# Retention's sums of squares as two float32r products of a high and a low part with ones

## The reference

```python
def head_layernorm(y):
    mu = jnp.mean(yf, axis=-1, keepdims=True)
    var = jnp.mean((yf - mu) ** 2, axis=-1, keepdims=True)
    return (yf - mu) * lax.rsqrt(var + EPS)
...
q = rope(q.reshape(B, S, H, d), cos, sin)
k = rope(k.reshape(B, S, H, d), cos, sin) * (d ** -0.5)
y_ret = head_layernorm(retention_chunkwise(q, k, v, log_gamma)).reshape(B, S, RET_WIDTH)
y_a = (jax.nn.silu(g_ret) * y_ret) @ ret_w_out[l]
```

## Time and profile before

| | us |
|---|---|
| median of 3 runs | 2533.19 (2532.08 to 2534.12) |
| the profiled execution | 2532.75 |
| its span, first to last instruction | 2531.0 |
| retention stage, first head's first score to the last head's root | about 1605 to 1821 |

### The profile page before, as it was taken

One profiled execution on the slowest core, in us unless ns is written; L12 is line 12 of the kernel. 1 busy time (PEld: TensorE's weight loads), 2 busy tenths in 40 slices (PEclk: granted clock), 3 DMA queues, 4 the chain that ended last, 5 costly groups with the idle time before them and its releaser, 6 DMA issues.

```text
span 2531.0 us, 35040 instructions
## 1 busy us (share of the span) xinstructions
PE 2474.6 (98%) x13577; PEld 2236.6 (88%) x13593; DVE 1825.4 (72%) x3334; ACT 1064.8 (42%) x1585; POOL 483.3 (19%) x344
## 2 busy tenths in 40 slices
PE   8999899999999999999999999999999999999998
PEld 6788888899999998999999999787788888888887
DVE  7876577999999989688888887787786335533323
ACT  6555366345555555333333335444422223422222
POOL 3222165033322353233333310000000000000000
PEclk9999999999999999999999999999999999999999
DMA  4211344588988899999999983222275333233231
GB/s 167 68 60 43 117 142 160 182 305 329 331 302 301 309 398 365 362 377 365 367 368 364 363 315 128 75 84 96 93 265 188 100 100 108 75 100 98 89 105 42
DMA packets 191236, 519.12 MB, mean 205 GB/s; under 512 B 15896, under 2 KB 67096, under 8 KB 187872
## 3 DMA queue, kind: packets, MB, share of 16 engines
q1 hardware_dynamic: 154208, 382.66, 43.2%
q0 software_dynamic: 36864, 134.23, 14.6%
HBM read 464.34 MB, written 52.49 MB: 204 GB/s over the span
## 4 chain that ended last, share of the span: by engine, by line
PE 81%; DVE 11%; DMA 4%; ACT 3%; issue 2%; SPq 0%; DVEq 0%; ACTq 0%
PE P L1240 25%; PE P L1242 25%; PE P L1241 24%; DMA GB<-un,SI 3%; DVE wl L1696 2%; PE P L1584 1%; PE P L1247 1%; DVE GB L2000 1%; ACT wh L2326 1%; DVE T L1696 1%; DVE D L1696 1%; DVE RQ L2211 0%; DVE RW L1696 0%; DVE RU L1696 0%; DVE OE L1696 0%
## 5 line engine op out<-in xcount | busy, mean ns | idle before, releaser
L1240 PE MATMUL P<-XH,wh 128*128 128x512 f32 (+2 forms) x2272 | 851.1, 375 | 9.4 <-DVE wl L1696 6.7
L1242 PE MATMUL P<-XH,wl 128*128 128x512 f32 (+2 forms) x2272 | 824.8, 363 | 0.0
L1241 PE MATMUL P<-XL,wh 128*128 128x512 f32 (+2 forms) x2272 | 824.2, 363 | 0.0
L1696 DVE TENSOR_TENSOR wl<-raw,wh 128x1024 fp32r<-128x1024 f32 x418 | 506.4, 1219 | 39.5 <-ACT wh L2326 39.5
L2326 ACT ACTIVATE wh<-raw 128x1024 fp32r<-128x1024 f32 x458 | 480.7, 1052 | 127.2 <-PE P L1242 125.7
L1240 PEld LDWEIGHTS P<-XH,wh 128*128 128x128 f32 x2272 | 429.3, 189 | 56.4 <-DVE wl L1696 10.3
L1242 PEld LDWEIGHTS P<-XH,wl 128*128 128x128 f32 x2272 | 428.2, 188 | 48.0
L1241 PEld LDWEIGHTS P<-XL,wh 128*128 128x128 f32 x2272 | 429.2, 189 | 42.5 <-issue 1.9
L1240 PE MATMUL P<-AH,wh 128*128 128x384 f32 x1024 | 343.7, 336 | 2.2 <-DVE wl L1696 1.7
L1242 PE MATMUL P<-AH,wl 128*128 128x384 f32 x1024 | 342.2, 334 | 0.0
L1241 PE MATMUL P<-AL,wh 128*128 128x384 f32 x1024 | 342.2, 334 | 0.0
(11 more groups left out here) (326 smaller groups left out, 3211.1 us busy)
## 6 DMA issues: line engine op xcount, KB each, us to landing
raw<-wts SPq DMA_DIRECT2D x211, 512.0 KB, 3.6
raw<-ut SPq DMA_DIRECT2D x128, 512.0 KB, 6.6
raw<-vt SPq DMA_DIRECT2D x128, 512.0 KB, 9.7
hdram<-HID SPq DMA_DIRECT2D x64, 384.0 KB, 4.7
gdram<-GS SPq DMA_DIRECT2D x24, 1024.0 KB, 6.3
GI<-gdram SPq DMA_DIRECT2D x16, 1536.0 KB, 13.1
HI<-hdram SPq DMA_DIRECT2D x32, 768.0 KB, 11.8
AWC<-adat SPq DMA_DIRECT2D x64, 256.0 KB, 5.4
```

Of the source, the lines that this page charges most:

```text
L1240: e.matmul(bank, wh[:, w], H, start=start, stop=False)
L1241: e.matmul(bank, wh[:, w], L, start=False, stop=False)
L1242: return e.matmul(bank, wl[:, w], H, start=False, stop=stop)
L1696: return e.tensor_tensor(dst, a, b, op)
```

## The change

`r_root`'s product with ones is no longer one float32 matmul but two in float32r that add up in the same bank: ones x high part and ones x low part of the squares. So:

- ScalarE, in `r_values`, after the square: it waits for its own square and copies `RSQ` to `RSQH` (float32r).
- VectorE, in a new piece `r_square`: it waits for that copy and subtracts, `RSQL` = `RSQ` - `RSQH`, in place of `RSQ`. In head 0 it also copies `ones` to `onesr` (128x128) once.
- TensorE, in `r_root`: it waits for `RSQL` instead of `RSQ`, then two matmuls.
- `retain` hands out `r_root` 6.4 tiles behind `r_values` instead of 5.2; the way from `r_values` to the end of the head stays 11.0 tiles.
- `RSQH` takes the place of `SRL`'s first part in memory, so VectorE's first `SRL` of a head also waits for the head before's sums.

```diff
--- before.py
+++ after.py
@@ -643,9 +643,11 @@
             yield ("r_low", h, 3)
             yield 6.0
             yield ("r_values", h)
-            yield 5.2
+            yield 3.0
+            yield ("r_square", h)
+            yield 3.4
             yield ("r_root", h)
-            yield 4.4
+            yield 3.2
             yield ("r_factor", h, 0)
             yield ("r_factor", h, 1)
             yield 1.4
@@ -885,6 +887,9 @@
         SRL = at("SRL", F + 85, [128, 1280], F32R)
         DM = [at(f"DM{i}", F + 94 + 2 * i, [128, T], F32) for i in range(2)]
         RSQ = at("RSQ", F + 98, [128, T], F32)
+        RSQL = at("RSQL", F + 98, [128, T], F32R)
+        RSQH = at("RSQH", F + 85, [128, T], F32R)
+        onesr = at("onesr", F + 100, [128, 128], F32R)
         R1 = TB[4]
 
 
@@ -969,7 +974,7 @@
         s_rope, s_qrh, s_qrl, s_rcopy = sem("s_rope"), sem("s_qrh"), sem("s_qrl"), sem("s_rcopy")
         s_rt, s_rcen, s_vrh, s_vrl, s_silu = sem("s_rt"), sem("s_rcen"), sem("s_vrh"), sem("s_vrl"), sem("s_silu")
         s_rsc, s_rdm, s_srh, s_srl = sem("s_rsc"), sem("s_rdm"), sem("s_srh"), sem("s_srl")
-        s_rval, s_rsq, s_rg, s_rones = sem("s_rval"), sem("s_rsq"), sem("s_rg"), sem("s_rones")
+        s_rval, s_rsq, s_rg, s_rsql, s_rones = sem("s_rval"), sem("s_rsq"), sem("s_rg"), sem("s_rsql"), sem("s_rones")
         s_rroot, s_rq = sem("s_rroot"), sem("s_rq")
         s_ry, s_rh, s_rl = sem("s_ry"), sem("s_rh"), sem("s_rl")
 
@@ -1648,8 +1653,9 @@
                     p.wait_ge(s_rroot, h)
                 else:
                     p.wait_ge(s_silu, 1)
-                p.wait_ge(s_rsq, h + 1)
-                e.matmul(P[5][:, :], ones[:, :], RSQ[:, :], start=True, stop=True).then_inc(s_rones, 1)
+                p.wait_ge(s_rsql, h + 1)
+                e.matmul(P[5][:, :], onesr[:, :], RSQH[:, :], start=True, stop=False)
+                e.matmul(P[5][:, :], onesr[:, :], RSQL[:, :], start=False, stop=True).then_inc(s_rones, 1)
 
             def down(m, k, u, c, half):
                 if c == 0:
@@ -2192,6 +2198,8 @@
                 w = T - 128 * kb
                 q = slice(offs[kb], offs[kb + 1])
                 v.wait_ge(s_srh, n + 1)
+                if h and kb == 0:
+                    v.wait_ge(s_rones, h)
                 tt(SRL[:, q], TB[5 + n % 2][:, 0:w], SRH[:, q].bitcast(F32), ALU.subtract).then_inc(s_srl, 1)
 
             def r_first(k):
@@ -2202,8 +2210,14 @@
             def r_values(h):
                 sg = TB[2 + h % 2]
                 v.wait_ge(s_silu, h + 1)
-                v.wait_ge(s_rsq, h + 1)
+                v.wait_ge(s_rsq, 2 * h + 1)
                 tt(sg[:, :], P[4][:, :], sg[:, :], ALU.mult).then_inc(s_rg, 1)
+
+            def r_square(h):
+                if h == 0:
+                    e.tensor_copy(onesr[:, :], ones[:, :])
+                v.wait_ge(s_rsq, 2 * h + 2)
+                tt(RSQL[:, :], RSQ[:, :], RSQH[:, :].bitcast(F32), ALU.subtract).then_inc(s_rsql, 1)
 
             def r_factor(h, half):
                 w = cols(half)
@@ -2310,7 +2324,7 @@
                 constants, slopes, gained, low, root, norm, norm_low, masks, forget, scaled, qk_split, v_copy, v_turn, soft, normal, turn_low,
                 values, mixed, subkeys, query, top, places, candidates, pair, gate, chosen, index, gate_turn, iotas, hot, weigh, angle,
                 rotation, rotation_end, mod_part, mod_end, rows, sparse_index, dot, dots_end, axpy, second, sum2, first_norm, rope, r_turn,
-                r_decay, r_low, r_first, r_values, r_factor, r_end, conv_begin, conv, merge_a, merge_b, merged, remixed,
+                r_decay, r_low, r_first, r_values, r_square, r_factor, r_end, conv_begin, conv, merge_a, merge_b, merged, remixed,
                 ffn_up, added, stored)}
             work |= {"sum": sum_, "activate": activate_}
             for name, *a in timeline():
@@ -2614,6 +2628,8 @@
                 if h:
                     c.wait_ge(s_rones, h)
                 e.activation(RSQ[:, :], P[4][:, :], ACT.Square).then_inc(s_rsq, 1)
+                c.wait_ge(s_rsq, 2 * h + 1)
+                copy(RSQH[:, :], RSQ[:, :]).then_inc(s_rsq, 1)
 
             def r_root(h):
                 c.wait_ge(s_rones, h + 1)
```

## The result

| | before | after |
|---|---|---|
| median of 20 runs each, us | 2533.31 | 2537.73 |
| the profiled execution, us | 2532.75 | 2535.82 |
| its span, us | 2531.0 | 2534.0 |
| from head 0's square to the end of the span, us | 905.55 | 909.25 |

The changed kernel takes 1.0021 of the time (95% interval 1.0015 to 1.0027). It is slower: the interval leaves out no change. The forecast was 2536.7, with the remark that such a loss would most likely be too small to be told from none; twenty runs of each kernel can just tell it.

The account below looks back on a forecast made before the run. ScalarE and VectorE, handing work round at 27.62 us per head, bound the retention, not TensorE. 3.45 + 1.58 - 0.68 - 0.41 = 3.9, less 0.2 in head 7, gives +3.7: 2536.7 us, 8-in-10 range 2533.5 to 2539.5.

Parts of the forecast that it names:

- The ring of ScalarE and VectorE: Retention heads: the two engines hand work to each other in a closed loop that sets the pace, 27.62 us per head.
- Rival 1: Retention: TensorE is the bound after all and keeps 3.3 us, time 2529.9, or 2528.4 without its waits; chance 0.10.
- VectorE's part: The added subtraction, pushing a weight unit by 0.60 us, falls into VectorE's 1.30 us wait for the root and costs nothing.
- The ring's growth: ScalarE's added copy lengthens each period from heads 1 to 5 by 0.69 us (bounds 0.54 and 0.88), 3.45 in all.
- Behind head 6: TensorE's work after head 6's sums: start 1.58 us later, less 0.68 for the moved tile and 0.41 for shorter products.
- The products: TensorE's sums in each head: two float32r products take 0.46 us instead of 0.87, a gain of 0.41.
- rival 3: Products with the float32r ones go at float32 pace, 1.28 us more per head than forecast, time 2539.3; chance 0.02.
- Head 0: ScalarE's copy of v there waits 1.46 us for TensorE, which covers the new copy, so no growth behind it.
- Head 7: Not paced by the other two engines: TensorE waits 0.2 us, saves 0.41, so 0.2 us gained.
- TensorE's waits: In front of the sums in each head, TensorE's wait becomes about 1.5 us, now for VectorE's `RSQL`.
- rival 2: The new waits let TensorE's clock fall, up to 7.9 us slower, 2539 to 2541; chance 0.10 that it decides.
- TensorE's own work: TensorE's work per head without waits: 27.24 us before, falling to 26.83, not what sets the pace.

Follow-up runs that it names:

- The copy alone: Kernel before plus only ScalarE's copy of the squares to float32r, unused, the sums still one float32 product; 2537.17 us (1.0010).
- one product: Changed kernel with squares written rounded to float32r, low part left out, one float32r product at its old place; 2532.28 us (0.9997).
- the move alone: Kernel before with only the sums product one tile later in TensorE's order; 2535.22 us (1.0004).
- the move undone: Changed kernel with the sums product back at its old place in TensorE's order; 2536.34 us (1.0007).
- the swap in before: Kernel before with each head's first-unit weight copy (ScalarE) and subtraction (VectorE) one tile later, behind the first masked scores; 2530.49 us (0.9986).
- the rounding on VectorE: Changed kernel with the high part of the squares copied by VectorE instead of ScalarE; 2536.81 us (1.0007).
- all three swaps: Weight copy and subtraction one tile later in kernel before, changed kernel, and changed kernel with high part on VectorE; 2530.49, 2530.93, 2529.45 us.

## Why the prediction was right, point by point

**The bound.** The ring of ScalarE and VectorE set the period, as the waits said. The copy alone gave the changed kernel's period with TensorE's work unchanged; one product left the period alone with TensorE's work cut by 0.64. Rival 1 is refuted by both. VectorE's part was free, as forecast.

**The ring's growth.** 0.66 us instead of 0.69. Both parts of the term were close: the copy started at +0.61 for +0.62, v's copy at +1.14 for +1.16. Over five periods it is 3.28 for 3.45. The 0.54 that a copy would cost without a lost overlap is excluded; the waiting instruction starts 0.03 us after the square's end, where an independent one starts 0.11 before it.

**Behind head 6.** I had 1.58 - 0.68 - 0.41 = +0.49, measured +0.52. The sums start at +2.35 for +2.30, which would make it 0.54; the other 0.02 is within the reading of the rows. The tile's 0.68 has its own run: 0.70 with the move alone, 0.59 with the move undone.

**The products.** In head 0, where TensorE doesn't wait, they take 0.23 each, so rival 3 falls; in heads 1 to 7, which come out of a stop, 0.54 together and not the 0.46 of the forecast. TensorE, head 0, after:

```profile
1628.66 0.39 PE L1657 MATMUL P<-RSQH,onesr 128*128 128x512 f32 x1
1628.89 0.39 PE L1658 MATMUL P<-RSQL,onesr 128*128 128x512 f32 x1
1629.12 0.39 PE L1245 MATMUL P<-XH,wh 128*128 128x512 f32 x1
```

**Head 0.** The interval behind it grew by 0.01: ScalarE's wait for TensorE did cover the copy.

**Head 7.** Here the sign was right and the size half: 0.11 gained for 0.2. All engines, from the square to the root, after:

```profile
1820.46 0.60 ACT L2630 ACTIVATE RSQ<-P 128x512 f32<-128x512 f32 x1 [3.71 <-PE P L1648]
...
1822.60 0.47 PE L1657 MATMUL P<-RSQH,onesr 128*128 128x512 f32 x1
1822.91 0.39 PE L1658 MATMUL P<-RSQL,onesr 128*128 128x512 f32 x1
1823.14 0.40 PE L1245 MATMUL P<-XH,wh 128*128 128x512 f32 x1
1823.34 0.69 ACT L2638 ACTIVATE RQ<-P,eps 128x512 f32<-128x512 f32 x1 [0.31 <-PE P L1658]
```

and the root in the kernel before:

```profile
1820.24 0.69 ACT L2622 ACTIVATE RQ<-P,eps 128x512 f32<-128x512 f32 x1 [1.06 <-PE P L1652]
```

From the square the root comes at +2.88 (1823.34 - 1820.46) for +2.96 (1820.24 - 1817.28). The products start at +2.14, 0.24 later than the old one, and the root follows 0.74 us behind that start, where it followed after 1.06 (1820.24 - 1819.18). So the products give back 0.32 and not 0.41. Most of what is missing is that the first of them now comes out of a stop: it takes 0.31 to the next start, not 0.23, which the old product, which found TensorE running, did not pay. My sum left that out. In head 6, the other one whose products count, it makes no difference, since the old product started from a stop there as well (its duration is 1.10 out of a stop in head 3, 1.02 without one in head 1). The root is thus 0.08 earlier; the other 0.03 of the 0.11 lie behind it, where two traces of the changed kernel differ by 0.01 and those of all kernels by up to 0.1.

**TensorE's waits and the clock.** Forecast about 1.5 us, measured 1.40 to 1.45 in heads 2 to 6 and 0.93 in head 1. The granted clock stayed at 1.00 from 1655 to 1793, so rival 2 did not come. No trace of the experiments shows a fall between head 0's square and 2517 us.

**TensorE's own work** was put too high: 27.24 us is the period less the recorded wait, but with the swap in before TensorE runs without a gap at 27.03. A stop costs more than its recorded wait. The matmul in front of the sums in head 3, before, is

```profile
1709.80 0.39 PE L1242 MATMUL P<-XH,wl 128*128 128x512 f32 x1
```

and the sums start 0.77 us behind its start, where a TensorE that runs takes 0.23: 0.54 lost for a recorded 0.38. With the 0.08 that the product is longer out of a stop, 27.62 - 0.54 - 0.08 = 27.00. In the changed kernel the same working gives 26.6 for the forecast's 26.83. The forecast of the wait is untouched, as the same overlap is left out on both sides of it, and so is the sum; but if TensorE's stops had gone under rival 1, that would have been worth about 3 us (5 x 0.59) and not 1.5.

**The sum.** 3.28 + 0.52 - 0.11 + 0.01 = 3.70, for 3.45 + 0.49 - 0.2 = 3.7. That it fits to the tenth is partly luck, as the ring was 0.17 too dear and the other terms 0.13 too cheap. The medians differ by 4.4 us; the 0.7 beyond the stretch's 3.70 is within what medians of one kernel differ by (2537.73 and 2536.54 for the changed one).

**What failed among the expectations** were three steps of mine behind the prediction: that a product's place changes TensorE's wait in every head; that the later start of the sums with the rounding on VectorE would cost nothing in the ring; and that GpSimd was free to use. In the swap in before, with 902.83 for an expected 904.0, there were two more: TensorE's own work, as above (five periods are 2.94 us shorter, where 27.25 would have made them 1.85 shorter), and that the interval from head 0 to head 1 shrinks too (28.25 from 29.19; it does so in all three swaps). Part of both comes back behind head 6 (25.76 from 24.56), as TensorE is then further behind ScalarE.

## What to carry to other kernels

- An engine that is busy 98% of the span need not set the pace of the stage that a change touches. Ask the waits view of that stage whether the other engines ever wait for it; if it is the one that waits, work taken from it turns into more waiting. Work given to the others is paid where their queue has no gap (ScalarE's copy, 0.66 us per head) and free where it falls into a wait of their own (VectorE's subtraction).
- Where engines hand work round in a ring, first shorten the ring, then the busy engine. The same two float32r products cost 3.7 us here and gain 0.4 once a weight copy has left ScalarE's part of the ring and the rounding is VectorE's.
- When a change is worth less than the scatter of the executions, measure it in the trace between two events that enclose it, and check that this repeats.

## What the runs showed of the hardware

- GpSimd's subtraction of 128x1024 (2.40 us, two inputs from SBUF) held up VectorE's subtraction of 128x512 from SBUF: 2.48 us for 0.69.
- VectorE rounds 128x512 from float32 to float32r in 0.41 us, ScalarE in 0.63.
- On ScalarE, waiting for the own forerunner's result cost 0.14 us: a start 0.03 us after its end for one 0.11 before it.
- Behind a stop, TensorE's first float32r matmul of 128x512 takes 0.31 us to the next start for 0.23, and the stop costs 0.16 us more than the wait that is recorded (0.77 between starts for a wait of 0.38).
- A TensorE that stopped for 1.4 us in every 28 kept its clock at 1.00 through the stage.
